# Memory keys and values as products of rounded parts in a two-block transformer kernel

## The reference, cut to what matters

```
x = x + 0.5 * swiglu(rms_norm(x, g_ffn1), w_ffn1_gu, w_ffn1_down)
proj = rms_norm(x, g_mix) @ w_in               # q, k, v of 12 heads "a" and 4 heads "b", 64 wide
oa = dilated_attention(qa, ka, va, bias_a)     # 12 heads
ob = moba_attention(qb, kb, vb, bias_b)        # 4 heads
ya, yb = rms_norm(oa, g_out_a), rms_norm(ob, g_out_b)     # over 768 and over 256 features
x = x + concatenate([ya, yb]) @ w_out
mn = rms_norm(mem, g_mem)                      # memory, 256 x 1024
k, v = split(mn @ w_ckv, 2)                    # 1024 columns each
x = x + softmax((rms_norm(x, g_cross) @ w_cq) k.T / 16) v @ w_co
x = x + 0.5 * swiglu(rms_norm(x, g_ffn2), w_ffn2_gu, w_ffn2_down)
```

## Time and profile before

| what | value |
|---|---|
| median of 3 runs | 1914.81 us (1913.39 to 1916.36) |
| the profiled execution | 1912.63 us, span 1910.8 us |
| mean granted clock of TensorE | 0.991 of full |
| PE busy | 98% of the span |
| DVE, ACT, POOL busy | 54%, 36%, 20% |
| data moved by DMA | 165.65 MB, 87 GB/s in the mean |

### The profile page before, as it was taken

How to read it: one execution, slowest core, us unless ns; L and a number is a source line. 1 busy time by engine, 2 the same in 40 slices (tenths; PEclk the granted TensorE clock), 3 DMA queues, 4 the chain that set the end, 5 groups by cost and what they waited for, 6 DMA issues and landing times.

```text
span 1910.8 us, 26251 instructions
## 1 busy us (share of the span) xinstructions
PE 1872.0 (98%) x9284; PEld 1473.2 (77%) x9284; DVE 1036.4 (54%) x2106; ACT 693.2 (36%) x1274; POOL 385.9 (20%) x223
## 2 busy tenths in 40 slices
PE   6999999999999999999999999999999999999998
PEld 4666777866677788888888777777887888888887
DVE  4589787558978756455533323333544655555322
ACT  3344444434444443323222243343323432233222
POOL 2335252433524240000000122220110100000000
PEclk8999999999999999999999999999999999999999
DMA  5222112222211233223323412222221223333332
GB/s 188 67 67 78 56 56 79 90 67 67 77 57 56 79 128 98 89 98 99 99 99 99 151 53 78 69 83 82 88 89 45 68 90 96 99 99 97 101 99 88
DMA packets 48577, 165.65 MB, mean 87 GB/s; under 512 B 5592, under 2 KB 6104, under 8 KB 48472
## 3 DMA queue, kind: packets, MB, share of 16 engines
q1 hardware_dynamic: 47176, 161.88, 26.4%
q10 hardware_dynamic: 1296, 2.42, 0.4%
HBM read 162.12 MB, written 2.17 MB: 86 GB/s over the span
## 4 chain that ended last, share of the span: by engine, by line
PE 91%; DVE 4%; issue 2%; ACT 1%; DMA 1%; POOL 1%; DVEq 0%; POOLq 0%; SPq 0%; ACTq 0%
PE proj L859 73%; PE score L1072 2%; PE o L1108 2%; PE turned L1084 2%; PE proj L1226 1%; PE proj L1230 1%; PE turned L1294 1%; PE score L1288 1%; PE o L1318 1%; PE turned L829 1%; PE score L961 1%; PE o L1382 1%; PE score L1371 1%; DVE wlo L1785 1%; PE turned L843 1%
## 5 line engine op out<-in xcount | busy, mean ns | idle before, releaser
L859 PE MATMUL proj<-hhi,whi 128*128 128x512 f32 x1488 | 601.9, 405 | 5.5 <-POOL wlo L652 2.6
L859 PE MATMUL proj<-hlo,whi 128*128 128x512 f32 x1488 | 584.0, 392 | 0.0
L859 PE MATMUL proj<-hhi,wlo 128*128 128x512 f32 x1488 | 583.8, 392 | 0.0
L1430 ACT ACTIVATE whi<-ring 128x1024 fp32r<-128x1024 f32 x266 | 281.4, 1058 | 679.8 <-PE proj L859 633.3
L859 PEld LDWEIGHTS proj<-hhi,whi 128*128 128x128 f32 x1488 | 281.8, 189 | 103.4 <-issue 35.8
L859 PEld LDWEIGHTS proj<-hhi,wlo 128*128 128x128 f32 x1488 | 281.7, 189 | 61.0
L859 PEld LDWEIGHTS proj<-hlo,whi 128*128 128x128 f32 x1488 | 282.2, 190 | 55.7 <-issue 1.0
L1785 DVE TENSOR_TENSOR wlo<-ring,whi 128x1024 fp32r<-128x1024 f32 x187 | 228.5, 1222 | 165.4 <-ACT whi L1430 165.3
L652 POOL TENSOR_TENSOR wlo<-ring,whi 128x1024 fp32r<-128x1024 f32 x79 | 189.7, 2403 | 456.6 <-ACT whi L1430 456.4
L665 POOL TENSOR_TENSOR prob<-prob 128x512 f32<-128x512 f32 x30 | 46.4, 1547 | 859.2 <-ACT prob L1426 858.8
L1456 ACT ACTIVATE prob<-prob,negmax 128x256 f32<-128x256 f32 (+3 forms) x208 | 114.4, 551 | 153.6 <-DVE negmax L1829 153.6
(11 more groups left out here) (212 smaller groups left out, 2205.4 us busy)
## 6 DMA issues: line engine op xcount, KB each, us to landing
ring<-wstream SPq DMA_DIRECT2D x288, 512.0 KB, 3.5
arena<-lines SPq DMA_DIRECT2D x28, 256.0 KB, 5.7
arena<-x ACTq DMA_DIRECT2D x4, 512.0 KB, 6.3
out<-arena SPq DMA_DIRECT2D x8, 256.0 KB, 2.9
arena<-mem SPq DMA_DIRECT2D x1, 1024.0 KB, 8.4
par<-params ACTq DMA_DIRECT2D x3, 74.0 KB, 1.9
arena<-hot SPq DMA_DIRECT2D x2, 85.0 KB
arena<-rope SPq DMA_DIRECT2D x1, 128.0 KB, 6.6
```

Source lines behind the costliest of these rows:

```text
L859: mm = pe.matmul(b, rounded(w), rounded(rhs(v, k)), start=(first and n == 0 and p == 0), stop=(last and n == len(blocks) - 1 and p == 2))
L1430: act.activation(rounded(dst), src, ACT.Copy, scale=scale).then_inc(ready, 1)
```

## The change

- Every KV slot is split like the others, the difference by DVE. The normed memory is split too: ACT writes `memhi`, DVE `memlo`, over `memT` and `memN`. A key job becomes 24 matmuls of 256 memory columns. Two value slots form one job (KV8 with KV9, and so on): the loads take two output blocks of 128 columns and half of the contraction each (`load_v`), so a value slot has 24 matmuls of 256 weight columns with the memory as weights, and one copy takes out both (512 columns).
- The planner's cost of a KV chunk is 0.34 instead of 0.45. Window 8 has KV8 to KV13; KV14 and KV15 come behind the steps.
- MSUM is cut into four parts that stand between Q2's chunks.
- The pairs go in the order 6, 7, 0, ..., 5, so the second group's heads are done first. For the first group's pairs, ACT squares y and rounds it with its gain as soon as it is there, and DVE makes the difference two steps later. The sums of squares are 4 tiles in place of 3.
- The root of the first group's mean is no longer in y: DVE evicts an output job with `tmp = proj * R` and adds `tmp` to `xT` (two operations in place of one), R being a copy of the first group's spread root. The second group's two tiles are scaled by the quotient of the two roots (its mean times the reciprocal of the other's).
- After the sums: KV15, then chunks 0 to 4 of OUT0, then the spreading, chunks 0 to 4 of OUT1, then the rest of OUT0 and OUT1.

```diff
+    ("KV8", "KV9", "KV10", "KV11", "KV12", "KV13"))
+KV_LAST = (14, 15)
+PAIR_ORDER = (6, 7, 0, 1, 2, 3, 4, 5)
+GROUP_B = 2
...
+            if name == "Q2":
+                for k in range(KC):
+                    pieces += [(name, k, 0.68)] + ([("MSUM", k // 2, 0.25)] if k % 2 == 0 else [])
+            elif name[:2] == "KV":
+                pieces += [(name, k, 0.34) for k in range(KC)]
...
+            def load_v(n):
+
+                u, block = (stream_of(n) - PAIR_AT - 4 * KC) % 2, stream_of(n) // 2 * 2
+                assert (PAIR_AT + 4 * KC) % 2 == 0
+                src = bass.AP(wstream.tensor, block * P * SLOT + u * 4 * P, [[SLOT, P], [P * SLOT, 2], [1, 4 * P]])
+                sp.dma_start(ring[:, n % RING, :].rearrange("p (b n) -> p b n", b=2), src).then_inc(wload[n % RING], 16)
...
                 if n < KC:
-                    mm = pe.matmul(b[:, 0:MEM], w[:, k * P:(k + 1) * P], memN[:, k, :], start=(k == 0), stop=(k == KC - 1))
+                    cols = slice(k * P, (k + 1) * P)
+                    for p, (w, v) in enumerate(((whi[:, h, cols], memhi), (whi[:, h, cols], memlo), (wlo[:, s, cols], memhi))):
+                        mm = pe.matmul(b[:, 0:MEM], rounded(w), rounded(v[:, k, :]), start=(k == 0 and p == 0),
+                                       stop=(k == KC - 1 and p == 2))
                 else:
-                    t = k // 4
-                    for i in range(2 * (k % 4), 2 * (k % 4) + 2):
-                        mm = pe.matmul(b[:, t * P:(t + 1) * P], memN[:, i, t * P:(t + 1) * P], w[:, i * P:(i + 1) * P],
-                                       start=(i == 0), stop=(i == KC - 1))
+                    u, t = n % 2, k // 4
+                    kk, tok = 4 * u + k % 4, slice(t * P, (t + 1) * P)
+                    for p, (w, v) in enumerate(((whi[:, h, :], memhi), (wlo[:, s, :], memhi), (whi[:, h, :], memlo))):
+                        wv = w.rearrange("p (b k n) -> p b k n", b=2, k=4)[:, :, k % 4, :]
+                        mm = pe.matmul(b[:, t * MEM:(t + 1) * MEM].rearrange("p (b n) -> p b n", b=2), rounded(v[:, kk, tok]),
+                                       rounded(wv), start=(u == 0 and k == 0 and p == 0), stop=False, skip_group_check=True)
...
+            kv_job(KV_LAST[0])
+            for n in range(GROUP_B):
+                add_squares(turned[0], NT, o2sqB[:, n, :], n == 0)
+            pe.wait_ge(o2sq_added, KC - GROUP_B - 2)
+            add_squares(turned[0], 0, o2sq[:, 0, :])
             pe.wait_ge(o2sq_ready, KC)
-            add_squares(turned[0], NT, sq[:, 0, :]).then_inc(o2sum_done, 1)
-            for n in range(KV_FILL, KV_MID):
-                kv_job(n)
+            add_squares(turned[0], 0, sq[:, 0, :]).then_inc(o2sum_done, 1)
+            kv_job(KV_LAST[1])
+            early = KC - GROUP_B - 1
+            mixout_chunks(0, range(early), True)
             pe.wait_ge(spread_ready, R_HEADS + 1)
             spread_roots(turned[1], spread[0][:, 0:NT, :])
             spread_roots(turned[0], spread[0][:, NT:2 * NT, :]).then_inc(spread_done, 1)
-            for n in range(KV_MID, 2 * KC):
-                kv_job(n)
+            mixout_chunks(1, range(early))
+            mixout_chunks(0, range(early, KC), True)
+            mixout_chunks(1, range(early, KC))
+            for c in range(2, KC):
+                mixout_chunks(c, range(KC))
...
+            heads_out(KC - 1)
+            after_mix(f"KV{KV_LAST[0]}")
+            after_mix(f"KV{KV_LAST[1]}")
+            make_high2(MIXOUT_AT)
+            make_high2(MIXOUT_AT + 1)
+            copy_R(SPREAD_NO[R_HEADS] + 1)
...
+            dve.wait_ge(heads_step, 1)
+            dve.reciprocal(ms[:, 2 * NT:3 * NT], ms[:, 0:NT]).then_inc(heads_step, 1)
+            dve.wait_ge(heads_step, 2)
+            dve.tensor_tensor(ms[:, NT:2 * NT], ms[:, NT:2 * NT], ms[:, 2 * NT:3 * NT], ALU.mult).then_inc(mean_ready, 1)
+            make_low2(MIXOUT_AT)
             spread_diag(R_HEADS, spread[0], range(2 * NT)).then_inc(spread_ready, 1)
+            make_low2(MIXOUT_AT + 1)
...
+            def residual_heads(c):
+
+                j = MIX_JOB[f"OUT{c}"]
+                dve.wait_ge(job_done, j + 1)
+                dve.tensor_tensor(tmp[:, c % 2, :], proj[j % 2][:, :], R[:, :], ALU.mult).then_inc(out_step, 1)
+                dve.wait_ge(out_step, c + 1)
+                dve.tensor_tensor(xT[:, c, :], xT[:, c, :], tmp[:, c % 2, :], ALU.add).then_inc(job_free[j % 2], 1)
```

More of the change, by code:

```diff
@@ L108 @@
     ("Q1", "MT0", "K1", "MT1", "MT2", "VT1", "MT3", "VN1"),
[L109 removed]
+    ("Q2", "K2", "VT2", "MROOT", "VN2"),
     ("Q3", "K3", "VT3", "KV0", "KV1", "VN3"),
@@ L114 @@
     ("Q7", "K7", "VT7", "KV7", "VN7"),
[L115 to L119, removed]
+    ("KV8", "KV9", "KV10", "KV11", "KV12", "KV13"))
+KV_LAST = (14, 15)
+PAIR_ORDER = (6, 7, 0, 1, 2, 3, 4, 5)
+GROUP_B = 2
+MIX_ORDER = ["Q0", "K0", "VT0", "VN0"] + [name for names in MIX_WINDOWS for part in names
+                                          for name in (("MSUM", part) if part == "Q2" else (part,))] \
+    + [f"KV{n}" for n in KV_LAST] + [f"{w}{c}" for w in ("OUT", "CQ", "CO") for c in range(KC)]
+V_FIRST = [f"KV{n}" for n in range(KC, 2 * KC, 2)]
+MIX_JOBS = [name for name in MIX_ORDER if name[:2] != "VN" and name not in V_FIRST]
 MIX_JOB = {name: FFN1_JOB + FFN_JOBS + n for n, name in enumerate(MIX_JOBS)}
+for _n in range(KC, 2 * KC, 2):
+    MIX_JOB[f"KV{_n}"] = MIX_JOB[f"KV{_n + 1}"]
 MIX_TAKE = [name for name in MIX_ORDER if name[:2] not in ("VN", "MT", "MS", "MR")]
@@ L143, in is_pair, with is_kv @@
     return PAIR_AT <= n < FFN2_AT and MIX_TAKE[n - PAIR_AT].rstrip("0123456789") in ("Q", "K", "VT")
+def is_kv(n, first=0):
+    return PAIR_AT <= n < FFN2_AT and MIX_TAKE[n - PAIR_AT][:2] == "KV" and int(MIX_TAKE[n - PAIR_AT][2:]) >= first
 def is_split(n):
@@ L149, in is_split @@
         return n % LAYER_SLOTS not in RAW
-    return not (PAIR_AT <= n < FFN2_AT and MIX_TAKE[n - PAIR_AT][:2] == "KV")
+    return True
 def on_pool(n):
@@ L1692, in after_mix @@
                 elif what == "KV":
-                    kv_copy(int(name[2:]))
+                    if name not in V_FIRST:
+                        kv_copy(int(name[2:]))
+                    if name in MIX_PREP:
+                        make_high2(MIX_PREP[name])
+                elif what == "MROOT":
+                    for c in range(KC):
+                        if c < KC - 1:
+                            act.wait_ge(memN_ready, c + 1)
+                        else:
+                            wait_out2(act, j)
+                        high(memN[:, c, :], memhi[:, c, :], memhi_ready)
                 elif what == "MT":
@@ L2292, in _ @@
                         spread_diag(R_MEM, spread[0], range(MEM // P)).then_inc(spread_ready, 1)
+                    if name == "MROOT":
+                        for c in range(KC):
+                            dve.wait_ge(memhi_ready, c + 1)
+                            dve.tensor_tensor(rounded(memlo[:, c, :]), memN[:, c, :], memhi[:, c, :], ALU.subtract)\
+                                .then_inc(memlo_ready, 1)
                 for name in MIX_ENDED[s] if s < MIX_STEPS else ():
                     after_mix(name)
+            low_heads(KC - 1)
```

155 lines of the change are left out of this document (86 added, 69 removed).

## The result

The changed kernel takes 1910.93 us in the median of 12 runs (1906.02 to 1912.44), the kernel before 1914.72 us beside it (12 runs, 1910.74 to 1916.36). The ratio is 0.998, with a 95% interval from 0.9971 to 0.9989: faster by 3.8 us, a third of the forecast 12. The same kernel in the first series of the experiments gave 1909.52 and 0.9981 (0.997 to 0.9992). The profiled execution took 1906.69 us, span 1904.9, so it is one of the quickest of the changed kernel, 5.9 us under the profiled one of before.

What follows compares the result with a forecast made beforehand. It took TensorE, busy 98% of the span, as the bound; -13.4 - 3.2 - 3.3 + 2.0 + 0.8 + 3.0 + 0.3 + 0.3 + 1.4 = -12.1 us, from 1912.63 to 1900.5 (median 1902.7), range 1896 to 1909.

Steps and rivals of the forecast that it cites:

- MSUM: One-column matmuls split between Q2's products: half clock goes, -3.6, a new wait adds +0.4, net -3.2 us.
- The gap behind KV15: At the mixing's end PE idles 3.0 us before OUT0, whose rounding and difference are queued behind KV15's copy.
- OUT2's late weights: Output jobs: OUT2's weights wait for OUT0's two-step eviction; PE waits 0.6 where before it waited 0.35, +0.3 us.
- the second rival: KV jobs: weight loads not hidden behind 256-column products, 0.223 each, +26.9 instead of -13.4, whole 1943 us; chance 0.04.
- The cost of a fall: Half clock after the new sums at the mixing's end: 0 to 3.4 us, taken as +2.0.
- the tail: Last steps of the mixing: DVE does KV14's and KV15's differences before step 31's row scaling, so the end is +1.4 us.
- The third rival: Mixing's end: clock stays at half through the new gap, costing about 7 us instead of 2, whole 1907.7; chance 0.08.
- the KV term: KV jobs as products of rounded parts: 384 matmuls at 0.118, 45.3 us instead of 58.7, so -13.4.
- The lateness of KV11: Last mixing steps: ACT does a step's exponentials and copy first, so KV11 is late by 0.3 us.
- the first rival: Preparing engines pace the KV jobs: nine places (Q4 to Q6, KV10 to KV15) lose 1.4 each, whole 1915.3; chance 0.08.
- the old end's half clock: The half clock at the old mixing's end, in the one-column sums and value matmuls behind them, goes: -3.3 us.
- the longer sums: At the mixing's end the sums become 32 instructions instead of 24: +0.8 us.

Runs made afterwards that it cites:

- after_again: The changed kernel run again with no edit: median 1909.52 us, 0.9981 of the kernel before.
- round_first: The changed kernel with OUT0's weights rounded on ACT ahead of the copy of KV15's result: 1905.34 us, 0.9961 of the kernel before.
- two_orders: The changed kernel with the edits of round_first and tail_order together: 1899.08 us, 0.9931 of the kernel before.
- all_three: The changed kernel with the edits of round_first, tail_order and spread_sums together: 1897.83 us, 0.9920 of the kernel before.
- spread_sums: The changed kernel with the heads' 32 one-column sums in four groups of 8 between KV14's and KV15's chunks: 1913.80 us, 0.9996 of the kernel before.
- all_three_block: all_three with MSUM's four parts in one run ahead of Q2 again: 1901.65 us, 0.9937 of the kernel before.
- tail_order: The changed kernel with DVE and ACT work behind KV12 and KV13 put after row scaling and turned-tile copies: 1907.10 us, 0.9965 of the kernel before.

## Why the prediction was wrong

**What held.** The direction; MSUM, forecast -3.2, is -3.2 at Q3 and 3.3 to 4.4 when undone. The gap behind KV15, forecast 3.0, is 2.94, with the cause given. The rounding is queued behind the copy, the difference behind that:

```profile
1346.05 0.60 ACT L1734 ACTIVATE arena<-proj 128x512 f32<-128x512 f32 x1 [9.04 <-PE proj L1265]
1346.54 1.99 ACT L1480 ACTIVATE whi<-ring 128x1024 fp32r<-128x1024 f32 x2
1347.62 1.23 DVE L1849 TENSOR_TENSOR wlo<-ring,whi 128x1024 fp32r<-128x1024 f32 x1 [5.41 <-ACT whi L1480]
```

OUT2's late weights: forecast 0.6, in the chain 0.7 from the end of OUT1's last nine products (2.06 behind the 24 that end at 1362.75) to 1365.54. Weight loads are hidden under 256 columns: the pace is 0.120, not the 0.223 of the second rival. The timeline, rows of key matmuls:

```profile
1174.36 0.39 PE L1258 MATMUL proj<-memhi,whi 128*128 128x256 f32 x1
1174.58 0.28 PE L1258 MATMUL proj<-memlo,whi 128*128 128x256 f32 x1
1174.70 0.27 PE L1258 MATMUL proj<-memhi,wlo 128*128 128x256 f32 x1
...
1178.52 0.28 PE L1258 MATMUL proj<-memlo,whi 128*128 128x256 f32 x1
1178.64 0.29 PE L1258 MATMUL proj<-memhi,wlo 128*128 128x256 f32 x1
```

The Trainium skill ("TensorE: Matmul & The Clock Gate", The mechanism; the prediction names the section behind it) states that only loads of another row group overlap with matmuls in flight, and in the same section that a load for the background weight buffer is pulled ahead as well. The first statement is not what this trace shows: full-height loads are hidden at a pace of 0.120. The second, which the prediction left out, agrees with it.

**The clock, the step that failed.** "The cost of a fall is 0 to 3.4 by the two old cases; I take 2.0." That took one fall, in the sums. The first profile has two, 1.6 + 3.1 = 4.7 us; that of after_again has one ahead of KV14, one in the sums and one behind the gap, 7.5. The extra falls come where TensorE waits and only small work stands around: the gap that I had counted, and the tail that I had lengthened. I put each wait down at its own length and gave the clock no price in them. round_first shows it for the gap (2.9 us of gap removed, 5.8 won in the profile, 3.8 in the ratio), two_orders for both (9.6 us by the ratios where the waits removed are 2.9 + 1.3).

The third rival, 1907.7 us, with a chance of 0.08, had a part of this: a clock that stays low through the gap, at about 7 us. In size that is near after_again's 7.5, though by another course (the clock rose in KV15 and fell again). It was too low by 3.2 because of the other terms: with the 2.8 us of the KV term and the 0.5 of the tail, both below, it gives 1911.0, and 1910.93 was measured. That it comes so near is in part luck, for the first profile has only 4.7 us of half clock and 1906.69.

**The KV term, mis-sized by as much.** Forecast -13.4 by 0.118 a matmul. The pace inside a job is 0.120, but the first matmul of each stretch takes 0.22, and steps cut the jobs in pieces: two key jobs take 1.43 + 4.50 = 5.93 where they took 2.59 + 4.51 = 7.10, so 0.59 a job, and a value job 2.99 instead of 3.73. The term is 8 x 0.59 + 8 x 0.74 = 10.6, 2.8 less than forecast: the new jobs cost 2.3 more than the 45.3 of the forecast, the old ones 0.5 less than its 58.7. The row that I used was six matmuls long, with another kind in front. In the first profile this is worth as much as the clock (4.7 - 2.0 = 2.7).

**The tail.** Forecast +1.4, measured 9.95 - 8.0 = +1.9. DVE's queue was the cause as written; it was free 6.7 us behind the scores instead of 6.0, and its second difference had waited 0.20 for ACT, which rounded KV15's weights behind KV13's copy. The lateness of KV11, forecast 0.3, didn't come, nor did a wait at any of the nine places of the first rival. PE waited 0.4 for POOL's difference at a tenth, Q7, which is prepared behind a KV job as Q4 to Q6 are and was not on the list:

```profile
1274.79 0.47 PE L889 MATMUL proj<-hhi,whi 128*128 128x512 f32 x1 [0.38 <-POOL wlo L682]
```

The sum with the measured terms (KV, MSUM, the old end's half clock, the new one's, the longer sums, the gap, Q7, OUT2, the tail): -10.6 - 3.2 - 3.3 + 4.7 + 0.8 + 2.9 + 0.4 + 0.4 + 1.9 = -6.0, against -5.9 of the two profiles. Stretch by stretch it fits less closely: +4.9 against a measured +4.4 from KV8 to T, -3.4 against -2.8 from T to OUT2. The rest to the medians (-3.8) is that the first profile of the changed kernel is one with little half clock: 1906.69 against a median of 1910.93, where before's was 1912.63 against 1914.72. So of the 8.3 us between forecast and medians, 2.8 are the KV term, 0.5 the tail, 2.7 the clock in the first profile, 0.2 small terms, and 2.1 what the median executions have over the profiled ones. after_again, with 2.8 us more of half clock than the first profile, says that this too is mostly the clock.

## What to carry to other kernels

Here a wait of TensorE near the end of dense work had two prices, its length and the half clock that could follow; look at the granted clock in the windows around every gap and every run of one-column matmuls before pricing an edit there. Where a change makes a helper engine serve a new item, put it behind what the critical engine waits for next: three reorderings with no work removed were worth 12 us here, three times the change itself. Where the executions of one kernel spread by more than the other's, take a second profile before explaining the first, and compare the stretch that the edit touches rather than whole executions: 246.9 against 255.6 us in one pair of profiles gave the 8.7 that the medians had blurred to 6.3.

## What the runs showed of the hardware

The same arrangement of matmuls ran at either level of the clock. Groups of 8 one-column matmuls between 6 products ran at 1.00 for 7.4 us in all_three, and at 0.50 from 1335.7 to 1353.0 in spread_sums, though TensorE was busy all that time; in after_again an undivided KV14 at 0.50 was followed by a rise.

32 one-column matmuls in one run did not always bring a fall. At MSUM the clock was 0.50 within the run in the kernel before, and still 1.00 at its end in all_three_block. At the end of the first block (704.8 us) it stayed at 1.00 in the first profile of the changed kernel, and was 0.66 and then 0.50 from 707 to 712 us in that of tail_order.

In after_again the clock also fell with TensorE not idle but waiting in pieces of 0.6 to 1.0 us between small matmuls: 1.00 from 1332.5 to 1333.6, then 0.59. In the first profile the same waits brought no fall. The same program did this in some executions and not in others; what decides was not found. The executions of spread_sums differ by up to 12 us (1903.75 to 1916.19), of which the stretch up to the end of the first block can account for about 2.
